# Level products of the WKV inverse on four array tiles, with the two head groups half a level apart

## The reference, cut to what matters

```
def step(state, inp):
    r_t, w_t, k_t, v_t, a_t, b_t = inp
    sa = jnp.einsum('bhvk,bhk->bhv', state, a_t)
    state = (state * w_t[:, :, None, :] + sa[..., None] * b_t[:, :, None, :]
             + v_t[..., None] * k_t[:, :, None, :])
    y = jnp.einsum('bhvk,bhk->bhv', state, r_t)
    return state, y
```

## Time and profile before

| | us |
|---|---|
| median of 3 runs | 2674.06 |
| lowest, highest | 2666.43, 2677.11 |
| the profiled execution's own time | 2677.45 |
| its span in the profile | 2675.6 |
| TensorE busy, of the span | 2374.8 (89%) |
| VectorE, ScalarE, GpSimd busy | 1099.5, 751.9, 390.1 |

### The profile page before, as it was taken

The page is one execution under the profiler, slowest core; times in us unless marked ns, Lnnn a source line. Parts: engine busy times, 40 slices in busy tenths (PEclk is TensorE's granted clock), DMA queues, the critical chain, the costliest instruction groups (busy, mean ns, idle before and its releaser), DMA issues. The chain is left out here.

```text
span 2675.6 us, 67587 instructions
## 1 busy us (share of the span) xinstructions
PE 2374.8 (89%) x27838; PEld 1461.8 (55%) x27839; DVE 1099.5 (41%) x2596; ACT 751.9 (28%) x1847; POOL 390.1 (15%) x480
## 2 busy tenths in 40 slices
PE   6999999999987899999999985599999999999960
PEld 5787877878766677776777763333332333332220
DVE  1455565655563455655556555111111111111118
ACT  1444545354441122231322220111221212221212
POOL 1112121112111121222212110001010111010000
PEclk8999999999997999999999996699999999999985
DMA  9111212112137422222222310935535496999959
GB/s 338 48 57 48 96 48 96 48 68 76 48 128 278 182 80 100 79 89 105 89 105 80 114 47 22 420 144 209 227 141 227 169 384 233 398 375 389 385 216 368
DMA packets 54244, 451.80 MB, mean 169 GB/s; under 512 B 7884, under 2 KB 8944, under 8 KB 32528
## 3 DMA queue, kind: packets, MB, share of 16 engines
q1 hardware_dynamic: 37656, 391.24, 37.4%
q0 software_dynamic: 10656, 38.80, 3.8%
q10 hardware_dynamic: 5720, 18.66, 1.8%
HBM read 367.41 MB, written 87.56 MB: 170 GB/s over the span
## 5 line engine op out<-in xcount | busy, mean ns | idle before, releaser
L1759 PE MATMUL ps<-arena 128*32 128x512 f32 x4608 | 513.0, 602 | 25.9 <-DMA arena<-wex 18.8
L443 PE MATMUL ps<-arena 128*128 128x128 f32 x3072 | 356.5, 277 | 14.3 <-ACT arena L589 14.3
L443 PEld LDWEIGHTS ps<-arena 128*128 128x128 f32 x3072 | 351.0, 193 | 27.1 <-ACT arena L589 24.5
L1759 PEld LDWEIGHTS ps<-arena 128*32 128x32 f32 x4608 | 150.4, 111 | 381.8 <-issue 367.0
L1099 PE MATMUL ps<-arena 64*64 64x64 f32 x8704 | 299.3, 222 | 30.5 <-issue 8.8
L1099 PEld LDWEIGHTS ps<-arena 64*64 64x64 f32 x8704 | 278.5, 136 | 60.3 <-issue 59.2
L1773 PE MATMUL ps<-arena 128*32 128x512 f32 x2304 | 268.3, 607 | 6.5 <-DMA arena<-wex 3.4
L1258 PE MATMUL ps<-arena 128*128 128x512 f32 x496 | 229.2, 605 | 0.7 <-ACT arena L1336 0.7
L1979 DVE TENSOR_TENSOR arena<-arena,ps 128x256 f32<-128x256 f32 x72 | 29.9, 415 | 466.7 <-ACT arena L1817 466.7
L458 PE MATMUL ps<-arena 128*128 128x512 f32 (+1 forms) x512 | 213.9, 555 | 0.0
L1817 ACT ACT_TABLE_LOAD x36 | 46.2, 1283 | 584.3 <-PE ps L1759 584.3
(11 more groups left out here) (331 smaller groups left out, 2836.5 us busy)
## 6 DMA issues: line engine op xcount, KB each, us to landing
arena<-wex SPq DMA_DIRECT2D x105, 2048.0 KB
mid<-arena SPq DMA_DIRECT2D x16, 2568.0 KB, 8.5
arena<-mid SPq DMA_DIRECT2D x16, 2568.0 KB, 9.7
arena<-ada SPq DMA_DIRECT2D x12, 2048.0 KB, 9.6
arena<-y SPq DMA_DIRECT2D x16, 1024.0 KB, 7.4
arena<-x SPq DMA_DIRECT2D x31, 512.0 KB, 5.6
arena<-x ACTq DMA_DIRECT2D x17, 512.0 KB, 10.3
arena<-w_in SPq DMA_DIRECT2D x4, 2048.0 KB, 39.0
```

The source lines that it names most:

```text
L443: mm = pe.matmul(bank[name][:, at:at + P], V["w_in"][g][:, kk, at:at + P], V["hT"][:, kk, :], start=(kk == 0), stop=(kk == KD - 1))
L1759: mm = pe.matmul(bank[("HA", "HB")[g]][rows[j], :], xT[:, kk, rows[j]], slot[j][:, at:at + 2 * FH], start=(kk == 0), stop=(kk == KD - 1))
```

## The change

What it does:

- The upper and lower halves of X, Z and ET are crossed: chunk q's X, ET and the first 64 columns of MT now lie in partition half 1 - q, while the transposed inverse and everything behind it stay in half q. For that the 128-column products of `M` with f = 0 become two of 64 columns each, into different halves.
- Level 0's transposed inverse is written to Z; `x2` makes both X and its transpose with identity products, in two banks.
- Each group has a bank for X (X0 or X1) and one for the transpose (YE or YO, the banks of y). `Xl` alternates, head by head, products with crossed halves (X) and with straight ones (transpose), so that four combinations of contraction half and output half follow one another. X is announced as full before the last two transpose products.
- ScalarE copies X and the transpose with an operation each (steps `X` and `T`).
- Z and X steps are per group, and the list puts group 1 half a level behind group 0. `x2_0`, `x2_1`, `Z1_0`, `X1_0` stand between output products; `h2T`, `route`, `res1`, `sq2`, `mean` move; `gn1` is split into three.

Its core:

```diff
-         "X0": ("M", "t0", *(f"x{l}" for l in _LV), "WT"),
-         "X1": ("M", "t0", *(f"x{l}" for l in _LV), "WT", "D0", "D1"),
-         "YE": ("y",), "YO": ("y",),
+         "X0": ("M", "t0", *(f"x{l}" for l in _LV[:-1]), "WT"),
+         "X1": ("M", "t0", *(f"x{l}" for l in _LV[:-1]), "WT", "D0", "D1"),
+         "YE": ("t0", *(f"x{l}" for l in _LV), "y"), "YO": ("t0", *(f"x{l}" for l in _LV), "y"),
...
+    X, XT = (lambda q, h: XX[chunk[1 - q], h // 4, 0, CHUNK * (h % 4):CHUNK * (h % 4) + CHUNK],
+             lambda q, h: XX[chunk[q], h // 4, 1, CHUNK * (h % 4):CHUNK * (h % 4) + CHUNK])
+    LEVEL_BANKS = (("X0", "YE"), ("X1", "YO"))
...
-    ORDER = (("Z2", 1), ("ss2", -1), ("X2", 1), ("mod2", 1), ("Z3", 1), ("norm2", -1), ("X3", 1), ("mod0", 1), ("mod3", 1),
-             ("h2T", -1), ("Z4", 1), ("h2", -1), ("X4", 1), ("mod4", 1), ("route", -1), ("Z5", 1), ("gn1", 0), ("X5", 1),
-             ("mod1", 1), ("mod5", 1), ("gn2", 0), ("Wg", 1), ("mod6", 1), ("Yv", 1), ("Wt", 1), ("mod7", 1),
-             ("Wi", 1), ("mod8", 1), ("yT", 0), ("load", 2), ("S0a", 1), ("o0", 0), ("o1", 0), ("S0b", 1), ("pick", -1), ("o2", 0),
-             ("o3", 0), ("S1a", 1), ("o4", 0), ("o5", 0), ("S1b", 1), ("Ma", 2), ("Mb", 2), ("mean", 1), ("o6", 0),
-             ("o7", 0), ("o8", 0), ("o9", 0), ("o10", 0), ("o11", 0), ("o12", 0), ("o13", 0), ("o14", 0), ("o15", 0),
-             ("weigh", -1), ("res0", 0), ("x2", 2), ("nrm", 1), ("Z1", 2), ("var", 1), ("res1", 0), ("X1", 2), ("sq2", 0))
+    ORDER = (("Z2_0", 1), ("X1_1", 1), ("res1", -1), ("X2_0", 1), ("T1_1", 1), ("T2_0", 1), ("sq2", -1), ("Z2_1", 1), ("mod2", 1),
+             ("Z3_0", 1), ("X2_1", 1), ("ss2", -1), ("gn1a", 0), ("X3_0", 1), ("T2_1", 1), ("T3_0", 1), ("Z3_1", 1), ("mod0", 1), ("mod3", 1),
+             ("Z4_0", 1), ("X3_1", 1), ("norm2", -1), ("X4_0", 1), ("T3_1", 1), ("T4_0", 1), ("Z4_1", 1), ("mod4", 1),
+             ("Z5_0", 1), ("X4_1", 1), ("gn1b", 0), ("X5_0", 1), ("T4_1", 1), ("T5_0", 1), ("Z5_1", 1), ("h2T", -1), ("X5_1", 1), ("T5_1", 1),
+             ("h2", -1), ("mod1", 1), ("mod5", 1), ("Wg", 1), ("mod6", 1), ("gn1c", 0), ("gn2", 0), ("Yv", 1), ("route", -1), ("Wt", 1),
+             ("mod7", 1), ("Wi", 1), ("mod8", 1), ("yT", 0), ("load", 2), ("S0a", 1), ("o0", 0), ("o1", 0), ("S0b", 1), ("pick", -1),
+             ("o2", 0), ("o3", 0), ("S1a", 1), ("o4", 0), ("o5", 0), ("S1b", 1), ("mean", 1), ("Ma", 2), ("Mb", 2), ("o6", 0), ("o7", 0),
+             ("o8", 0), ("o9", 0), ("x2_0", 2), ("o10", 0), ("x2_1", 2), ("o11", 0), ("o12", 0), ("o13", 0), ("weigh", -1), ("res0", 0),
+             ("nrm", 1), ("Z1_0", 2), ("o14", 0), ("o15", 0), ("var", 1), ("X1_0", 2), ("T1_0", 2), ("Z1_1", 2))
...
+                                    to = 256 * i + 128 * f
+                                    if f == 0:
+                                        pe.matmul(bank[name][chunk[1 - q], to:to + CHUNK], pk[key][hd, at:at + CHUNK],
+                                                  pk["AR"][hd, c, 0, chunk[q]], start=True, stop=True)
+                                        pe.matmul(bank[name][chunk[q], to + CHUNK:to + 2 * CHUNK], pk[key][hd, at:at + CHUNK],
+                                                  pk["AR"][hd, c, 1, chunk[q]], start=True, stop=True)
+                                        continue
...
+            def x2(g):
...
+                    for h in range(4 * g, 4 * g + 4):
+                        for r in range(2):
+                            mm = pe.matmul(level_out(LEVEL_BANKS[g][0], r, h), Z[chunk[r], h, :], k("ident64")[chunk[r], :],
+                                           start=True, stop=True)
+                            if h % 4 == 3 and r == 1:
+                                B.full(mm, LEVEL_BANKS[g][0])
+                        for r in range(2):
+                            mm = pe.matmul(level_out(LEVEL_BANKS[g][1], 1 - r, h), k("ident64")[chunk[r], :], Z[chunk[r], h, :],
+                                           start=True, stop=True)
+                    B.full(mm, LEVEL_BANKS[g][1])
...
+                    blocks(f"Z{g}", lambda q, h: ET[l][chunk[1 - q], h, :], X, range(4 * g, 4 * g + 4))
...
-                        if l < last:
-                            blocks(f"X{g}", XT, lambda rows, h: Z[rows, h, :], heads, last=False)
-                        blocks(f"X{g}", lambda rows, h: Z[rows, h, :], XT, heads, at=256, first=(l == last))
+                    for h in range(4 * g, 4 * g + 4):
                         if l < last:
+                            for q in range(2):
+                                mm = pe.matmul(level_out(own, 1 - q, h), XT(q, h), Z[chunk[q], h, :], start=True, stop=True)
+                            if h % 4 == 3:
+                                B.full(mm, own)
+                        for q in range(2):
+                            mm = pe.matmul(level_out(turned, q, h), Z[chunk[q], h, :], XT(q, h), start=True, stop=True)
+                    B.full(mm, turned)
...
-                        B.free(act.activation(XX[:, g, o:, :], split(bank[f"X{g}"][:, 256 * o:], 2 - o), ACT.Copy), f"X{g}")
+                    B.wait_full(act, name, f"x{l}", n)
+                    B.free(act.activation(XX[:, g, o, :], bank[name][:, 0:256], ACT.Copy), name)
```

More of the change, by code:

```diff
@@ L1091, in M, with blocks, level_out, go @@
                 return go
-            def blocks(name, lhs, rhs, heads, at=0, first=True, last=True):
-                if first:
-                    pe.sem_inc(S["pe_passed"], 1)
[L1097 to L1102, removed]
-            def x2(n, b):
-                for g in range(2):
-                    S.wait(pe, "xt2", 2 * n + g + 1)
-                    B.wait_free(pe, f"X{g}", "t0", n)
-                    blocks(f"X{g}", XT, lambda rows, h: k("ident64")[rows, :], range(4 * g, 4 * g + 4))
-            def Zl(l):
+            def blocks(name, lhs, rhs, heads):
+                pe.sem_inc(S["pe_passed"], 1)
+                for i, h in enumerate(heads):
+                    for q in range(2):
+                        mm = pe.matmul(bank[name][chunk[q], CHUNK * i:CHUNK * i + CHUNK], lhs(q, h), rhs(q, h),
+                                       start=True, stop=True)
+                B.full(mm, name)
+            def level_out(name, half, h):
+                return bank[name][chunk[half], CHUNK * (h % 4):CHUNK * (h % 4) + CHUNK]
+            def x2(g):
+                def go(n, b):
+                    S.wait(pe, "xt2", 2 * n + g + 1)
+                    for name in LEVEL_BANKS[g]:
+                        B.wait_free(pe, name, "t0", n)
+                    pe.sem_inc(S["pe_passed"], 1)
+                    for h in range(4 * g, 4 * g + 4):
[6 more added lines that the diff above has]
+                            mm = pe.matmul(level_out(LEVEL_BANKS[g][1], 1 - r, h), k("ident64")[chunk[r], :], Z[chunk[r], h, :],
+                                           start=True, stop=True)
+                    B.full(mm, LEVEL_BANKS[g][1])
+                return go
+            def Zl(l, g):
                 def go(n, b):
@@ L1135, in Wg @@
                 B.wait_free(pe, "Z0", "G", n)
-                blocks("Z0", lambda rows, h: MT[rows, h, 128:192], lambda rows, h: pk["V"][rows, hs(h)], range(H))
+                blocks("Z0", lambda q, h: MT[chunk[q], h, 128:192], lambda q, h: pk["V"][chunk[q], hs(h)], range(H))
             def Wt(n, b):
@@ L1140, in Wt @@
                 for g in range(2):
-                    B.wait_read(pe, f"X{g}", f"x{last}", n)
+                    B.wait_read(pe, LEVEL_BANKS[g][1], f"x{last}", n)
                 for q in range(2):
@@ L1155, in Wi @@
                 B.wait_free(pe, "Z1", "I", n)
-                blocks("Z1", XT, lambda rows, h: W["G"][rows, hs(h)], range(H))
+                blocks("Z1", XT, lambda q, h: W["G"][chunk[q], hs(h)], range(H))
             def Yv(n, b):
@@ L1357, in weigh @@
                 act.activation(W["de"], W["dd"], ACT.Exp).then_inc(S["de"], 1)
-            run(act, {"x2": x2, **{f"X{l}": Xl(l) for l in _LV}, "Wg": Wg, "Wt": Wt, "nrm": nrm, "yT": yT, "sq2": norm2, "h2": h2T, "pick": pick, "weigh": weigh})
+            run(act, {"x2_1": x2, **{f"X{l}_{g}": level(l, g, 0) for l in range(1, last) for g in range(2)},
+                      **{f"T{l}_{g}": level(l, g, 1) for l in _LV for g in range(2)}, "Wg": Wg, "Wt": Wt, "nrm": nrm, "yT": yT, "sq2": norm2, "h2": h2T, "pick": pick, "weigh": weigh})
         @block.gpsimd
```

70 lines of the change are left out of this document (36 added, 34 removed).

## The result

The changed kernel takes 2704.15 us (median of 4 runs, 2700.34 to 2717.14), the kernel before 2670.24 beside it on the same chip: a ratio of 1.012, with a 95% interval of 1.0094 to 1.0146. The forecast was 2642 us, with a range up to 2665. The kernel is slower, so the sign was wrong. The profiled execution took 2700.34 us, with a span of 2698.5, 22.9 more than before.

What follows compares the result with a forecast made beforehand. TensorE's issue and its short waits were taken to bound the steady tile. 0.6 + 1.8 - 0.3 = 2.1 us a tile over 14 tiles, plus 3 for tiles 0 and 1, gave 32 us off 2674.06: 2642, range 2612 to 2665.

Steps and rivals of the forecast that it cites:

- instruction supply: TensorE: 128 records need some 3.7 us, levels 2 to 4 just below that; 0.3 us a tile charged for levels and masks.
- Rival (b): Supply binds throughout, 3.7 us or more per 128 records in levels, masks and W; gain 0.9 us a tile, 2659, chance 0.16.
- Rival (d): The clock falls because TensorE waits a quarter of each level; half rate costs 6 us a tile, 2760, chance 0.03.
- The four-tile rate: New X products rotating through four tiles take 15 to 16 ns a record: 32 records in 0.49 us instead of 0.93.
- Rival (c): The four-tile rate doesn't come about, 29 ns a record instead of 15; -1.6 us a tile, 2696, chance 0.05.
- The masks' products: Before level 2, 16 products of 128 columns become 32 of 64; taken as +0.1 us, bounds 0 and +0.9.
- The split of the output products and the stretch up to level 2: Output matmuls split 8/2/6/4 records, 0.15 us each shape change; first output record to Z of level 2 12.5 us, was 13.2.
- From there to Z of level 5: Levels 2 to 5, groups half a level apart: Z of level 5 starts 7.8 us after Z of level 2, was 13.0.
- From level 5 to the y transposes: h2's transposes, level 5, V, y, router, W and I take 9.9 us to the y transposes, where the old has 6.5.
- the sum of the parts: Gains of a steady tile: 0.6 us before level 2 plus 1.8 for levels 2 to 5 and after.
- Tiles 0 and 1, and the tail: Tiles 0 and 1, paced by adaLN loads or at mixed clock, gain 1.5 us each, 3 together; nothing for the tail.
- a tile of 44.4 us: Length forecast for a steady tile, the whole forecast in one number; wrong if a tile period stays above 46.

Runs made afterwards that it cites:

- w_repeated: The kernel before, with W's 16 four-tile products made 12 times in a row: 2837.46 us, ratio 1.0625.
- w_waits: w_repeated with a real wait on a ScalarE copy after the 4th and the 8th repetition: 2853.4 us.
- straight_tiles: The changed kernel with nothing crossed, level products on two tiles instead of four, masks' products not split: 2708.5 us, ratio 1.0126.
- old_order: The changed kernel with the list of steps of the kernel before, its new steps in their places: 2694.91 us, ratio 1.0099.
- after_late_residual: The changed kernel with the 512 KB residual load issued at o0 instead of at the y transposes: 2692.83 us, ratio 1.0093.
- masks_whole: The changed kernel with the crossing turned round so the masks' products stay unsplit, 64 instructions fewer a tile: 2703.44 us, ratio 1.0116.
- before_late_residual: The kernel before with only the residual's load issued at o0 instead of at the y transposes: 2673.61 us, ratio 0.9996.

## Why the prediction was wrong, point by point

**The step that failed: instruction supply.** It took 3.7 us for 128 records as a limit, compared it with 3.5 us of the new levels, and charged 0.3 us a tile beyond today's stalls. The limit was right for an uninterrupted run (3.47 to 3.75 in w_repeated). The charge was not: stalls cost 2.2 us a tile more. What stands in place of the fixed 3.7 us is a packet that comes late by an amount that varies. In an uninterrupted run it starts 1.1 to 1.7 us behind the boundary, in the changed kernel up to 3.97 us in the levels (the block from 1246.22 us, 6.28 us long) and 4.25 in the V and y products behind them (from 1202.28). A level isn't an uninterrupted run: TensorE waits at semaphores in it, and w_waits shows that a wait can delay a packet, by some 1 us when it comes within the first 22 instructions. And "just below the limit" was no margin: once the levels ask for a block about as fast as it comes, there is little slack to hide a late packet in. straight_tiles, which asks for them more slowly, has a third of the stalls. Rival (b) had named this cause, but priced the blocks at the same 3.7 us, 0.9 us a tile.

Why the packets are late in the levels stays open. In a third of the blocks of the changed kernel that began with a stall (10 of 33), and in most of old_order's (28 of 35), no wait of over 0.08 us is recorded between the boundary and the packet, and packets are late there too, by medians of 2.19 and 2.08 us. The block with the latest packet of all, +4.25 us, is one of them. In the others the first wait stands mostly at places that w_waits didn't test, and the 1 us that it measured is less than the largest delays here (2 to 3 us beyond those of the uninterrupted run). So waits are one cause that can be shown in a test, but not shown to be the one in the levels.

**The clock.** Rival (d), at 0.03, had every level product at half rate. What came is smaller and has another trigger: seven stretches of 3.4 us at half clock in the twelve steady tiles, of which six begin within 1.5 us of the end of a gap of 2.0 us or more (two of them at 1202.7 and 1253.9 us, behind 1202.28 and 1252.49). Not every such gap brings one: behind 2.47 us that end at 1394.66 the clock stays at 1.00. By the fit the stretches cost 0.6 us a tile. The Trainium skill ("TensorE: Matmul & The Clock Gate", Part 1) ties the clock to how busy TensorE was; the windows at 1249 and 1253.87 agree. My evidence against (d), was a stretch whose waits were short, and said nothing of a standstill of 2.7 us.

**The steps that held.** The four-tile rate: 32 records of W start in 0.51 us (1259.45 to 1259.96), 32 of X of level 1 in 0.52 (1236.91 to 1237.43), 16 ns each. Rival (c) is out. The masks' products take 2.13 us, from 1223.54 to 1225.67, against 1.89 before (1214.35 to 1216.24): +0.24 where the sum had +0.1. The split of the output products and the stretch up to level 2:

```profile
1229.93 1.13 PE L1291 MATMUL ps<-arena 128*128 128x512 f32 x2
1231.61 2.84 PE L1291 MATMUL ps<-arena 128*128 128x512 f32 x6
1234.38 0.68 PE L1109 MATMUL ps<-arena 64*64 64x64 f32 x16
1234.99 1.99 PE L1291 MATMUL ps<-arena 128*128 128x512 f32 x4
```

From the first of them at 1225.67 to Z of level 2 at 1237.90 (16 records of 29 ns behind 1237.43) it is 12.2 us; the forecast was 12.5, and before it was 13.2. From there to Z of level 5 (1247.33) it is 9.4 us, 1.3 of it stalls: 8.1 against 7.8. From level 5 to the y transposes 13.7 us, of which 2.67 are the stall and 1.5 the half clock in the V and y products: 9.5 against 9.9. So in this tile the sum of the parts, 2.4 us before the charge, was nearly right where nothing stalls. The fit over twelve tiles has 1.7, so some 0.7 us of the gain may be missing besides the stalls. (The prediction's 17.8 us for levels and after should be 7.8 + 9.9 = 17.7; that moves nothing.)

**Tiles 0 and 1, and the tail.** The forecast was -3 and 0; measured were +6.4 and +3.2. In the first the granted clock was lower too, 0.80 over the 182 us instead of 0.87 over 176, and in after_late_residual the late load alone gave 6.4 back there. I had taken these tiles as paced by the adaLN loads, and the sum had no term for anything that lengthens them; what did is not shown. For the tail I had named no mechanism and have none now.

**The forecast as a whole.** The summary number, a tile of 44.4 us, is close to the base of the fit, 44.25. That closeness is partly luck: the forecast started from one tile of 46.5 us, where twelve have a mean of 46.75 and a base without stalls of 45.93, and it added 0.3 us for stalls where 2.2 came. Stalls and clock made 47.82 of it.

## What to carry to other kernels

Where a kernel issues many small products, count TensorE's instructions between two boundaries and compare with 3.5 us for 256 of them, and take this as the best case: a wait at a semaphore within the first 22 instructions of a block wasn't hidden in the refill but came on top of it. Products that run faster (four tiles instead of two) gain little once the stretch is near that limit: here 0.8 us a tile of 2.8. Fewer and wider products gained 11 us in the kernel before, half of it in issue stalls, and nothing in the changed one. And a new idle time of some 2 us can be followed by half the granted clock in the work behind it, so that it belongs in a sum with more than its own length.

## What the runs showed of the hardware

- TensorE's instructions come in packets of 16 KB, one for each 256 loads, matmuls and semaphore instructions. That one block is reserve at most is an inference: instructions saved ahead of the dense stretch (masks_whole) saved nothing in it.
- A stall at the boundary ends 2.2 to 2.9 us after the packet's start. In an uninterrupted run the packet starts 1.1 to 1.7 us behind the boundary; with a wait within the first 22 instructions 1.95 to 2.23 us.
- Which packets are late is mostly set by the program: between the kernel before and before_late_residual, the delays of 105 packets behind their boundaries agree with a correlation of 0.975.
- From 1.4 us behind a standstill of 2.67 us the granted clock was 0.51 for 3.4 us, with TensorE busy all the time; 64-column records came every 53 ns on two tiles instead of every 29.
